# A quarter of the value table's low parts made by GpSimd, and TensorE's low passes one step later

## What is computed

```python
def peer_ffn(xn, wq, sub_keys, u_tab, v_tab):        # u_tab, v_tab (16384, 2048)
    ...                                             # 8 heads; each token gets 16 experts of 16384 per head
    gates = jax.nn.softmax(cand_v, axis=-1)
    def block(args):
        xb, eb, gb = args
        act = jax.nn.gelu(jnp.einsum('td,tkd->tk', xb, u_tab[eb]))
        return jnp.einsum('tk,tkd->td', gb * act, v_tab[eb])
```

## Time and profile before

| | |
|---|---|
| median of 3 runs | 2738.12 us (2737.78 to 2738.59) |
| profiled execution | 2745.46 us, span 2743.7 us |
| mean granted clock of TensorE | 0.896 |
| TensorE busy | 2211.6 us (81%) |
| VectorE busy | 2101.2 us (77%) |
| ScalarE busy | 1239.0 us (45%) |
| GpSimd busy | 719.9 us (26%) |
| DMA, mean over the span | 266 GB/s |

### The profile page before, as it was taken

The page is one execution under the profiler, slowest core; times in us unless marked ns, Lnnn a source line. Parts: engine busy times, 40 slices in busy tenths (PEclk is TensorE's granted clock), DMA queues, the critical chain, the costliest instruction groups (busy, mean ns, idle before and its releaser), DMA issues.

```text
span 2743.7 us, 38575 instructions
## 1 busy us (share of the span) xinstructions
PE 2211.6 (81%) x14161; PEld 1999.5 (73%) x14161; DVE 2101.2 (77%) x2789; ACT 1239.0 (45%) x1930; POOL 719.9 (26%) x395
## 2 busy tenths in 40 slices
PE   7999999999999999999999500003338999999997
PEld 6989999999999888899889400002337777777776
DVE  6786555656654755664468999999999999999998
ACT  4555544444444443454355200046954444444444
POOL 0000000000000100010002586886894442424330
PEclk9999999999999999999999755555559999999999
DMA  6544565554566466564457897999977999999996
GB/s 203 165 134 132 179 182 174 154 153 146 160 200 177 146 207 191 174 196 153 137 177 290 333 392 307 394 395 402 396 284 283 422 421 422 421 421 422 422 422 244
DMA packets 325176, 729.36 MB, mean 266 GB/s; under 512 B 23256, under 2 KB 265136, under 8 KB 267072
## 3 DMA queue, kind: packets, MB, share of 16 engines
q1 hardware_dynamic: 277648, 386.18, 41.8%
q0 software_dynamic: 46912, 340.81, 31.0%
q10 hardware_dynamic: 496, 0.84, 0.1%
HBM read 725.66 MB, written 2.10 MB: 265 GB/s over the span
## 4 chain that ended last, share of the span: by engine, by line
PE 54%; DVE 27%; DMA 11%; issue 7%; ACT 1%; SPq 1%; POOL 0%; DVEq 0%; ACTq 0%; POOLq 0%
PE bank L412 34%; DVE b_u_ring L2105 13%; PE bank L445 12%; DMA b_late_row<-in_peer_u,b_idx_all 6%; DMA b_late_row<-in_peer_v,b_idx_all 5%; DVE b_v_lo L2157 3%; PE bank L1659 2%; PE bank L1441 1%; DVE b_hN L2181 1%; PE bank L1326 1%; DVE b_late_row L2174 1%; DVE b_oct_rows L2147 1%; DVE b_w_both L391 1%; DVE b_e_parts L2162 1%; SPq L679 1%
## 5 line engine op out<-in xcount | busy, mean ns | idle before, releaser
L391 DVE TENSOR_TENSOR b_w_both<-b_raw,b_w_both 128x1024 fp32r<-128x1024 f32 x464 | 569.0, 1244 | 452.8 <-ACT b_w_both L386 451.5
L386 ACT ACTIVATE b_w_both<-b_raw 128x1024 fp32r<-128x1024 f32 x464 | 484.2, 1057 | 570.4 <-PE bank L412 380.7
L412 PE MATMUL bank<-b_act_both,b_w_both 128*128 128x256 f32 x4224 | 516.6, 284 | 2.7 <-ACT b_w_both L386 2.7
L412 PEld LDWEIGHTS bank<-b_act_both,b_w_both 128*128 128x128 f32 x4224 | 510.4, 192 | 4.8 <-ACT b_w_both L386 3.1
L769 POOL DMA_INDIRECT b_u_ring<-in_peer_u,b_idx_all x192 | 416.6, 2170 | 158.8 <-DVE b_dots L2105 82.5
L2105 DVE CUSTOM_DVE_ANT_0 b_u_ring<-b_u_ring,b_xnN 128x2048 f32<-128x2048 f32 x192 | 437.2, 2281 | 0.0
L1218 ACT ACTIVATE b_v_hi<-b_v_raw 128x1024 fp32r<-128x1024 f32 x256 | 271.9, 1062 | 340.5 <-PE bank L1659 191.8
L1659 PE MATMUL bank<-b_v_hi,b_e_parts 128*128 128x512 f32 x1536 | 397.7, 395 | 0.0
L412 PE MATMUL bank<-b_att_both,b_w_both 128*128 128x256 f32 x3072 | 375.1, 284 | 0.0
L412 PEld LDWEIGHTS bank<-b_att_both,b_w_both 128*128 128x128 f32 x3072 | 371.6, 193 | 0.6 <-issue 0.5
L1659 PEld LDWEIGHTS bank<-b_v_hi,b_e_parts 128*128 128x128 f32 x1536 | 293.1, 191 | 64.2 <-ACT b_v_hi L1218 0.4
(11 more groups left out here) (327 smaller groups left out, 2262.4 us busy)
## 6 DMA issues: line engine op xcount, KB each, us to landing
b_v_raw<-in_peer_v SPq DMA_DIRECT2D x128, 1024.0 KB
b_raw<-in_w_in SPq DMA_DIRECT2D x208, 512.0 KB, 4.6
b_raw<-in_w_proj_dsa SPq DMA_DIRECT2D x32, 512.0 KB, 3.6
b_raw<-in_w_proj_gla SPq DMA_DIRECT2D x32, 512.0 KB, 3.5
b_raw<-in_w_xk SPq DMA_DIRECT2D x32, 512.0 KB, 4.8
b_raw<-in_w_out SPq DMA_DIRECT2D x32, 512.0 KB, 3.5
b_raw<-in_w_xv SPq DMA_DIRECT2D x32, 512.0 KB, 4.6
b_raw<-in_w_xq SPq DMA_DIRECT2D x32, 512.0 KB, 3.5
```

Of the source, the lines that this page charges most:

```text
L386: act.activation(w_hi[:, q], raw[:, UQ * c + q], ACT.Copy).then_inc(w_high, 1)
L391: dve.tensor_tensor(w_lo[:, q], raw[:, UQ * c + q], w_hi[:, q].bitcast(F32), ALU.subtract).then_inc(w_split, 1)
L412: mm = pe.matmul(proj[c][:, n], lhs, rhs, start=(q == 0 and n == 0 and k == 0 and w is w_hi and x is hi), stop=(q == UQ - 1 and k == UK - ...
```

## The change

GpSimd makes the low part of half tiles 3, 7, 11, ... 255 (n % 4 == 3), VectorE those of the other 192. There are now two semaphores: `v_split` counts VectorE's low parts and `v_split_pool` GpSimd's; `low_made(eng, n, before)` waits for that of half tile n. SyncE waits for both halves of the tile that it writes over, ScalarE for that of half tile n - 2, TensorE for its own.

On GpSimd's queue the late rows and the low parts are laid in one order. Ahead of low part n, those rows are issued whose place comes free in step n - 2 or earlier (`freed_at`); the others come behind it.

TensorE makes high pass n + 1 ahead of low pass n; one high pass stands ahead of the loop. The number of instructions of each kind and all transfers stay as they are.

```diff
+POOL_LOW = 3
+    def low_by_pool(n):
+        return n % 4 == POOL_LOW
+    def low_made(eng, n, before=0):
+        if low_by_pool(n):
+            eng.wait_ge(sem("v_split_pool"), before + n // 4 + 1)
+        else:
+            eng.wait_ge(sem("v_split"), before * 3 + n // 4 * 3 + n % 4 - (n % 4 > POOL_LOW) + 1)
+    def freed_at(m):
+        if m in ROWS_GROW:
+            return PER_BATCH * (ROWS_GROW[m] - 2) + 3
+        return LATE_FROM + LATE_SPAN * (m - row_back[m]) // LATE_ROWS if m >= 3 else 0
...
             if j >= 4:
-                sp.wait_ge(sem("v_split"), 2 * (j - tile_back[j]) + 2)
+                for n in (2 * (j - tile_back[j]), 2 * (j - tile_back[j]) + 1):
+                    low_made(sp, n)
...
-        late_rows(2, LATE_ROWS)
+        def value_low(n):
+            pool.wait_ge(sem("v_high"), n + 1)
+            if n == POOL_LOW:
+                pool.wait_ge(sem("seeded"), 2)
+            if n >= 4:
+                pool.wait_ge(sem("v_used"), n - 3)
+            pool.tensor_tensor(v_lo[n % 4], raw_half(n), v_hi[:, n % 2].bitcast(F32), ALU.subtract).then_inc(sem("v_split_pool"), 1)
+
+        row = 2
+        for n in range(POOL_LOW, STEPS, 4):
+            while row < LATE_ROWS and freed_at(row) < n - 1:
+                late_rows(row, row + 1)
+                row += 1
+            value_low(n)
+        late_rows(row, LATE_ROWS)
...
                 act.wait_ge(sem("v_high_used"), n - 1)
-                act.wait_ge(sem("v_split"), n - 1)
+                low_made(act, n - 2)
...
+        def high_pass(b, n):
+            if n % PER_BATCH == 0:
+                pe.wait_ge(sem("e_split"), b * 2 + n // PER_BATCH + 1)
+            pe.wait_ge(sem("v_high"), b * 4 * BATCH + n + 1)
+            slot, i, v = n // PER_BATCH % 2, n // 2 % BATCH, n % 2
+            for e in (E_HI, E_LO, E_SHARED):
+                for m in range(2):
+                    mm = pe.matmul(...)
+            mm.then_inc(sem("v_high_used"), 1)
+        def low_pass(b, n, last=False):
+            low_made(pe, n, b * BATCH)
+            ...
+            mm.then_inc(sem("v_used"), 1)
         def values(b, last=False):
             for n in range(4 * BATCH):
+                if not (last and n == 4 * BATCH - 1):
+                    high_pass(b, n + 1)
+                low_pass(b, n, last)
...
+        high_pass(0, 0)
         with pe.Fori(0, NKEYS // (2 * BATCH) - 1) as b:
             values(b)
...
         for n in range(STEPS):
             if n % PER_BATCH == 3 and n // PER_BATCH + 1 < NKEYS // BATCH:
                 weights_low(n // PER_BATCH + 1)
-            value_low(n)
+            if not low_by_pool(n):
+                value_low(n)
             for m in late_at(n):
                 late_step(m)
```

More of the change, by code:

```diff
@@ L711, in _ @@
             if j >= 4:
-                sp.wait_ge(sem("v_split"), 2 * (j - tile_back[j]) + 2)
+                for n in (2 * (j - tile_back[j]), 2 * (j - tile_back[j]) + 1):
+                    low_made(sp, n)
             where, count = landed(v_landed, tile_place, j)
             sp.dma_start(v_raw[tile_place[j]], v_rows[j * P:(j + 1) * P]).then_inc(where, 16)
-        sp.wait_ge(sem("v_split"), 2 * NKEYS)
+        for n in (STEPS - 2, STEPS - 1):
+            low_made(sp, n)
         sp.dma_start(gfin, a["norm_final_g"].partition_broadcast(P)).then_inc(sem("final_gain_landed"), 16)
@@ L1644, in seed @@
             return mm
+        def high_pass(b, n):
[5 more added lines that the diff above has]
+                for m in range(2):
+                    mm = pe.matmul(bank[(4 if e is E_SHARED else 0) + 2 * v + m], e_parts[:, slot, i, e],
+                                   v_hi[:, v, m * 512:(m + 1) * 512], start=False, stop=False, skip_group_check=True)
+            mm.then_inc(sem("v_high_used"), 1)
@@ new lines, in low_pass @@
+        def low_pass(b, n, last=False):
+            low_made(pe, n, b * BATCH)
+            slot, i, v = n // PER_BATCH % 2, n // 2 % BATCH, n % 2
+            for e in (E_SHARED, E_HI):
+                for m in range(2):
+                    mm = pe.matmul(bank[(4 if e is E_SHARED else 0) + 2 * v + m], e_parts[:, slot, i, e],
+                                   v_lo[n % 4][:, m * 512:(m + 1) * 512], start=False, stop=(last and n >= 4 * BATCH - 2),
+                                   skip_group_check=True)
+            mm.then_inc(sem("v_used"), 1)
```

## The result

| | before | after |
|---|---|---|
| median, 5 runs each | 2738.59 us | 2803.72 us |
| ratio after / before | | 1.0231 (95%: 1.0206 to 1.0256), +63 us |
| profiled execution | 2745.46 us | 2800.84 us |
| VectorE busy, whole kernel | 2101.2 us | 2158.9 us |
| GpSimd busy, whole kernel | 719.9 us | 876.8 us |

What follows compares the result with a forecast made beforehand. Transfers and VectorE were taken as limits 4% apart, VectorE to become the bound: 607.0 - 70.4 + 136.4 + 6 = 679 us for the first stretch instead of 631, +48, so 2786 us; range 2757 to 2812.

Steps and rivals of the forecast that it cites:

- Two limits 4% apart: Value stage: VectorE and the transfers are both nearly full; a faster DMA gains at most 24 us, a faster VectorE little.
- Part 1: VectorE up to half tile 247: 62 low parts of 1.135 us leave it, -70.4 us.
- Part 2: Value stage: each GpSimd subtraction costs VectorE 2.2 us, 62 times, +136.4 us.
- One sign that I named: Value stage: mean low part, dot and row sum of VectorE grow by about 2.2 us in total per GpSimd subtraction.
- The engines alternate: VectorE stands still while GpSimd subtracts, 2.26 us of each period in an earlier place of the trace.
- Part 3: VectorE's idle time in the first stretch: row waits go, high-part waits stay; 6 us, bounds 0 and 24.
- Part 4: TensorE's low pass n behind high pass n+1 removes most of its 99 us of waits, worth 0 in time.
- Part 5: End of the kernel: shorter remaining TensorE work against a later last fold, together 0, from -2 to +3 us.
- The sum: First stretch 679 us instead of 631, +48; median 2786 us.
- The first: Rival: GpSimd works beside VectorE at no charge and transfers alone set the pace; 2733 us, chance 0.10.
- The second: Rival: the hold on VectorE is real but partly covered, 1.7 us each; 2755 us, chance 0.12.
- The third: Rival: longer pauses make TensorE's clock fall to half rate repeatedly, +50 us, 2836 us; chance 0.10.

Runs made afterwards that it cites:

- left_out: Changed kernel with GpSimd making only half tile 3's low part and nobody the rest of its share; ratio 0.9997 to the kernel before.
- one_input: Changed kernel with GpSimd copying the raw half tile into its low part instead of subtracting; ratio 0.9979 to the kernel before.
- every_eighth: Changed kernel with GpSimd making the low part of every eighth half tile, 32 instead of 64; ratio 1.0081 to the kernel before.
- order_alone: Changed kernel with all low parts back on VectorE, so only TensorE's order is new; ratio 1.0001 to the kernel before.
- pool_alone: Changed kernel with TensorE in its old order, GpSimd still making a quarter of the low parts; ratio 1.0229 to the kernel before.
- phase_1: Changed kernel with GpSimd taking half tiles 1, 5, 9, ... 253 instead of 3, 7, ... 255; ratio 1.018 to the kernel before.

## Why the prediction was right, step by step

- *Two limits 4% apart, and only a heavier VectorE matters.* Right, and shown from both sides: left_out (a lighter VectorE) 0.9997, one_input 0.9979, the change 1.0231.
- *Part 1, -70.4 us.* Right in the count, 507 instructions instead of 570. left_out has VectorE busy 59.7 us less in the middle 600 us, where 59 low parts at 1.135 us would be 67; why it is less is open.
- *Part 2, a hold of 2.2 us.* Right in kind, 0.1 us low in size. From the busy times of the first stretch, (679.0 - 606.9 + 70.4) / 62 = 2.30 us: +142.5 instead of +136.4, 6 us of the miss; by durations, which do not rest on the 70.4, it is 2.25. One sign that I named did not show: no dot of the changed kernel is longer (2293 ns at the most, as before), and nine tenths of the loss fall on the low parts of the weights. That is this kernel's phase and not a property of the dot: the one of every_eighth above lost 1.55 us, and in one_input dots take 2385 ns on the mean. In these profiles the instruction that is running when GpSimd comes mostly goes on, and the one that begins beside GpSimd's pays. "The engines alternate" was too strict as well. At 2760 us VectorE ran four instructions ahead of a waiting GpSimd:

```profile
2760.27 2.34 DVE L2227 SCALAR_TENSOR_TENSOR b_hN<-b_late_row,b_w_all,b_hN 128x2048 f32<-128x2048 f32 x1
2762.53 0.41 DVE L2208 TENSOR_TENSOR b_e_parts<-b_spread,b_e_parts 128x256 fp32r<-128x256 f32 x1
2762.86 0.28 DVE L2208 TENSOR_TENSOR b_e_parts<-b_spread_shared,b_e_parts 128x128 fp32r<-128x128 f32 x1
2763.07 1.22 DVE L2203 TENSOR_TENSOR b_v_lo<-b_v_raw,b_v_hi 128x1024 fp32r<-128x1024 f32 x1
2767.72 1.23 DVE L2203 TENSOR_TENSOR b_v_lo<-b_v_raw,b_v_hi 128x1024 fp32r<-128x1024 f32 x1 [3.44 <-ACT b_v_hi L1251]
...
2760.47 6.05 POOL L835 TENSOR_TENSOR b_v_lo<-b_v_raw,b_v_hi 128x1024 fp32r<-128x1024 f32 x1 [6.27 <-ACT b_v_hi L1251]
```

- *Part 3, 6 us of idle time.* This term was mis-sized: 692.7 - 679.0 = 13.7 us, 8 us of the miss. The six lines above show one way that I had no price for. VectorE worked on until 2764.3, GpSimd's part came only at 2766.5, ScalarE's high part waited for it, and VectorE stood 3.44 us for that high part. The hold is then not added to VectorE's instructions but waited for. Such waits for high parts were 12.5 us of the 13.7: 2.3 at the start of the stage, 3.4 before 2234.4, 4.5 before 2258.7, where GpSimd had issued gathers ahead of its subtraction, and 2.3 of this last one. Gone as said are the waits for rows (0.9 us); the rate, forecast at 386 GB/s, was 378.
- *Part 4, TensorE's order worth 0.* Right: order_alone 1.0001, and pool_alone against the change 1.0229 and 1.0231.
- *Part 5, the end, 0.* Right: 18.4 us from low pass 247 to TensorE's end instead of 19.4, and 14.3 instead of 13.3 from there to the end of the span.
- *The sum.* Forecast +48, measured +62.2 in the first stretch. Of the 14 us between them 6 are the hold's and 8 the idle time's. Both errors went the same way, and the result lies in the range, 15 us from its middle forecast. No large errors cancelled.
- *Rivals.* The first (no charge) is out by left_out, which shows what it would have been. The second (1.7 us, partly covered) is close to what the other phase and every_eighth show of VectorE's durations, 1.79 and 1.85, but not the kernel itself (2.25). The third is out: granted clock 0.97 in the stage, as before.

## What to carry to other kernels

Before work is moved from VectorE to an idle GpSimd, look in the trace for places where both work at once, and charge VectorE with the time that it lost there: here a subtraction that cost VectorE 1.135 us cost it 2.3 us when GpSimd made it. Here, where the transfer rate stood at its ceiling for the whole stage, relief of VectorE was worth nothing that could be measured clearly (0.9997, 0.9979), and only its burden counted. Leaving a moved operation out altogether shows what the move could gain at best, and the rest is its price.

## What the runs showed of the hardware

- The price of a GpSimd elementwise instruction for a VectorE that is busy almost without a break grows with its columns: 2.25 us for 1024 fp32 columns and two inputs, 1.73 for 768, 1.28 for 512; 0.97 for 1024 with one input (excess of VectorE's durations, for each). GpSimd's own shortest times are 2.35, 1.81, 1.27 and 1.04 us, so nearly all of its time is taken from VectorE. With GpSimd on other half tiles, or on half as many, it was 1.79 and 1.85.
- Small two-input subtractions of VectorE lasted up to 3.15 us. In the changed kernel GpSimd came into the middle of a dot (custom instruction, 2.28 us) and its instruction stretched to 4.17 us beside it. A dot that began beside a running GpSimd subtraction was itself lengthened, to 3.83 us in every_eighth and to 4.47 in phase_1.
- At 2408.27 VectorE's instruction already stood 0.57 us before GpSimd's is recorded as begun, and in pool_alone a dot lasted 4.95 us though GpSimd's subtraction is recorded as begun 0.37 us after it. Whether the record or the hold is early isn't settled.
- All that VectorE does at length in this stage reads two tensors. What an instruction with one would lose, and whether it is reading or writing that the two engines can't do at once, no run here shows.
